# Eight projection chunks in three passes over split operands, and the modulation chunks moved with them

## The reference, cut to what matters

```python
hc = modulate(rms_norm(ctx, norm1_g[l]), csh1, csc1)
s_f, s_b = context_states(hc @ w_in[l][:, HG_KDIM:3 * HG_KDIM + HG_WIDTH], lbs[l])
hx = modulate(rms_norm(x, norm1_g[l]), sh1, sc1)
x_mix, _, _ = token_mixer(hx @ w_in[l], lbs[l], s_f, s_b, *mix_args)
...
q, z_f, z_b, vi, g, p_hy, g_logits = jnp.split(p, SPLIT_POINTS, axis=-1)
o, s_f, s_b = hgrn2_bidir(heads(q...), heads(vi...), fwd, bwd, s0_f, s0_b)   # scans both ways, chunks of 32
y_a = hgrn2_readout(o, g, hg_norm_g, p.dtype)
y_b = hyena_branch(p_hy, conv_w, conv_b, filt, d_skip)
return merge_branches(y_a, y_b, g_logits, w_pa, w_pb, w_o), s_f, s_b
```

## Time and profile before

| what | value |
|---|---|
| median of 3 runs | 2048.84 us (2046.73 to 2051.15) |
| profiled execution: span of its instructions | 2045.0 us |
| TensorE busy | 1947.3 us, 95% of the span |
| "projected", from chunk 4 on | 153.8 to 234.9 us |
| the two scans | 234.9 to 276.4 and 276.4 to 313.0 us |
| "hyena" | 313.0 to 374.2 us |

### The profile page before, as it was taken

One profiled execution on the slowest core, in us unless ns is written; L12 is line 12 of the kernel. 1 busy time (PEld: TensorE's weight loads), 2 busy tenths in 40 slices (PEclk: granted clock), 3 DMA queues, 4 the chain that ended last, 5 costly groups with the idle time before them and its releaser, 6 DMA issues.

```text
span 2045.0 us, 27442 instructions
## 1 busy us (share of the span) xinstructions
PE 1947.3 (95%) x11522; PEld 1406.8 (69%) x11522; DVE 727.9 (36%) x1213; ACT 610.7 (30%) x931; POOL 389.3 (19%) x205
## 2 busy tenths in 40 slices
PE   6999899999999999997999799999999999988998
PEld 2767696864444444446887557777777778678998
DVE  1624244232222222226243744222222535464333
ACT  2422102032222222223112534322223511545454
POOL 2000000020000000005001321433333310424764
PEclk9999999989999999998999899999999999989999
DMA  9469916549999999982222102544444223414551
GB/s 360 162 219 363 336 42 226 191 169 394 428 423 426 423 426 422 425 353 89 102 105 95 62 31 107 181 144 144 170 159 144 84 82 124 167 42 142 188 176 52
DMA packets 120213, 428.38 MB, mean 209 GB/s; under 512 B 5690, under 2 KB 23141, under 8 KB 107456
## 3 DMA queue, kind: packets, MB, share of 16 engines
q1 hardware_dynamic: 118016, 416.56, 52.8%
q0 software_dynamic: 2112, 10.57, 1.4%
HBM read 426.07 MB, written 1.05 MB: 209 GB/s over the span
## 4 chain that ended last, share of the span: by engine, by line
PE 64%; PEld 18%; issue 6%; DVE 3%; POOL 2%; ACT 2%; DMA 2%; PEldq 0%; DVEq 0%; POOLq 0%; SPq 0%; ACTq 0%
PE bank L527 63%; PEld bank L527 18%; PE bank L542 2%; DMA ring<-in_ada_w 1%; DMA ring<-in_w_in 1%; PEldq L506 0%; POOL arena L1815 0%; POOL arena L1814 0%; DVE H L1900 0%; DVE H_low L1907 0%; DVE arena L2399 0%; POOL arena L1819 0%; POOL arena L1817 0%; POOL arena L1820 0%; POOL arena_r L1855 0%
## 5 line engine op out<-in xcount | busy, mean ns | idle before, releaser
L527 PE MATMUL bank<-arena_r 128*128 128x512 f32 (+1 forms) x2112 | 599.0, 351 | 11.8 <-ACT arena_r L1332 5.4
L527 PE MATMUL bank<-arena_r,ring_low 128*128 128x512 f32 (+2 forms) x1792 | 561.7, 348 | 5.4 <-DVE H_low L1907 5.3
L527 PEld LDWEIGHTS bank<-arena_r 128*128 128x128 f32 x2112 | 374.1, 190 | 103.9 <-issue 47.7
L527 PEld LDWEIGHTS bank<-arena_r,ring_low 128*128 128x128 f32 (+1 forms) x1792 | 329.2, 189 | 51.5 <-issue 6.1
L527 PE MATMUL bank<-arena 128*128 128x64 bf16 (+8 forms) x2588 | 308.6, 285 | 25.3 <-DMA arena<-in_hy_filt_w 11.3
L527 PEld LDWEIGHTS bank<-arena 128*128 128x128 bf16 (+4 forms) x2588 | 190.3, 132 | 129.6 <-issue 93.4
L527 PE MATMUL bank<-ring,arena 128*64 128x512 f32 x1024 | 278.2, 595 | 1.1 <-ACT arena L1501 0.7
L527 PE MATMUL bank<-H_low,arena_r 128*128 128x512 f32 (+1 forms) x672 | 217.6, 341 | 0.0
L2455 DVE SCALAR_TENSOR_TENSOR X<-bank,mod,X 128x256 f32<-128x256 f32 x216 | 94.6, 479 | 314.2 <-PE bank L527 314.2
L1346 ACT ACTIVATE arena<-bank 128x512 f32<-128x512 f32 (+2 forms) x106 | 51.4, 496 | 410.2 <-PE bank L527 410.1
L1841 POOL TENSOR_TENSOR ring_low<-ring,arena_r 128x2048 fp32r<-128x2048 f32 x32 | 146.9, 4613 | 141.3 <-ACT arena_r L1691 70.8
...
## 6 DMA issues: line engine op xcount, KB each, us to landing
...
H<-in_moe_w_down SPq DMA_DIRECT2D x16, 2048.0 KB, 15.9
...
```

The lines of the kernel that those rows point to most:

```text
L527: ins = nc.tensor.matmul(o, l, r, start=start, stop=stop, skip_group_check=True)
```

## The change

Projection chunks 4 to 11 are also done in three passes over split operands. For chunks 4 to 7 ScalarE copies the high half of the chunk (two pieces of 2048 columns, `first_high`) into `W4h`, of which chunks 5, 6 and 7 share one buffer, and GpSimd subtracts it from the slot into `ring_low` (`first_low`). TensorE does all high passes of the four tiles of a chunk first, and then the low ones. For gate chunks 8 to 11 the high half goes into the `ring_low` buffer of the next slot number, so that a gate chunk takes two numbers of the ring (`gate_high`, `gate_low`, `chunk_used(2)`). The latents are kept as two halves, `HPX` (tokens, in `X_r`) and `HPC` (context, in `arena_r`); the copy `HX` is gone, and a k-step of the two wide chunks has five matmuls (four of 256 columns, one of 512) in place of three of 512 (`wide3`). Scan scratch moves to free `W4h`: `QD` is written over `LC`, and so waits for `ctx_arg`. The modulation chunks are grouped anew: 14 are behind chunks 1 to 7 (16 before), four behind gate chunk 10 in one row and two behind gate chunk 11. The start of `scan_prep` waits for the high passes of chunk 4. A few semaphores are merged and renamed, which changes no order.

```diff
-        ADA1, WIN, MERGE, MOE = 0, 4, 36, 40
+        ADA1, WIN, MERGE, MOE = 0, 4, 40, 44
...
-        BEHIND = [[], [0], [1, 2], [3, 4, 5], [6, 7], [8, 9], [10, 11, 12], [13, 14, 15]]
+        BEHIND = [[], [0, 1], [2, 3], [4, 5], [6, 7], [8, 9], [10, 11], [12, 13]]
+        GROUP = [(4, 6, 0, 8)] * 8 + [(5, 7, 8, 6)] * 6 + [(6, 6, 14, 6)] * 6
         ADA_COLS = 384
 
         def win(j):
 
-            return WIN + j + sum(len(b) for b in BEHIND[:j]) if j < 8 else WIN + (24, 25, 28, 30)[j - 8]
-
-        GATE_ADA = [WIN + 26, WIN + 27, WIN + 29, WIN + 31]
+            return WIN + j + sum(len(b) for b in BEHIND[:j]) if j < 8 else WIN + (22, 24, 26, 32)[j - 8]
+
+        GATE_ADA = {14: WIN + 28, 15: WIN + 29, 16: WIN + 30, 17: WIN + 31, 18: WIN + 34, 19: WIN + 35}
...
-                for i in BEHIND[j] if j < 8 else ([], [16, 17], [18], [19])[j - 8]:
-                    n += 1
+                for i in BEHIND[j] if j < 8 else ([], [], [14, 15, 16, 17], [18, 19])[j - 8]:
+                    n = n + 1 if j < 8 else GATE_ADA[i]
...
-        Hw = H[:, :, :].rearrange("p k n -> p (k n)")
-        QM, KM, QD = [[A3(off, HG_H, L), Hw[:, h:h + 1024].rearrange("p (a b) -> p a b", a=HG_H)]
-                      for off, h in ((15360, 0), (16384, 1024), (17408, 2048))]
-        SC = [A3(18432, 8, P), Hw[:, 3072:4096].rearrange("p (a b) -> p a b", a=8)]
+        QM = [A3(15360, HG_H, L), H[:, 0:HG_H, L:2 * L]]
+        KM = [A3(16384, HG_H, L), H[:, HG_H:2 * HG_H, L:2 * L]]
+        QD = LC
+        SC = [A3(18432, 8, P), A3(17408, 8, P)]
...
-        Hp = AR3(12288, KT, 2 * L)
+        HPX, HPC = Xr[:, :, L:2 * L], AR3(12288, KT, L)
+        Hp = lambda k, s: (HPX, HPC)[s][:, k, :]
...
+        W4h = [ar_r[:, 14336:18432], ar_r[:, 19456:23552]]
...
+            def wide3(o, w, k, start, stop, inc=None):
+
+                mm(o[:, 0:L], w[0], HPX[:, k, :], start, False)
+                mm(o[:, L:2 * L], w[0], HPC[:, k, :], False, False)
+                mm(o, w[0], Hl[:, k, :], False, False)
+                mm(o[:, 0:L], w[1], HPX[:, k, :], False, False)
+                mm(o[:, L:2 * L], w[1], HPC[:, k, :], False, stop, inc)
+
+            def behind(n, i):
+                g, bank, first, V = GROUP[i]
+                ada(n, g, bank, i - first, V, blk=min(i // 8, 1))
...
+            def high_passes(o, wh, nts, inc=None):
+                for nt in nts:
+                    for k in range(KT):
+                        last = (nt, k) == (nts[-1], KT - 1)
+                        mm(o[nt][:, 0:L], wh[:, k, nt * P:(nt + 1) * P], HPX[:, k, :], k == 0, False)
+                        mm(o[nt][:, 0:L], wh[:, k, nt * P:(nt + 1) * P], Hl[:, k, 0:L], False, False, inc if last else None)
+
+            def low_passes(o, wl, nts):
+                for nt in nts:
+                    for k in range(KT):
+                        mm(o[nt][:, 0:L], wl[:, k, nt * P:(nt + 1) * P], HPX[:, k, :], False, k == KT - 1,
+                           "tile_done" if k == KT - 1 else None)
+
+            for j in range(4, 8):
+                n = win(j)
+                pe.wait_ge(S("first_high"), 2 * (j - 4) + 2)
+                o = [tile_bank() for nt in range(4)]
+                high_passes(o, W4h[min(j - 4, 1)].rearrange("p (k n) -> p k n", k=KT), range(4), "high_used")
+                if j == 5:
+                    ada_turn(4, 6, 0, 8)
+                pe.wait_ge(S("first_low"), 2 * (j - 4) + 2)
+                low_passes(o, as_cols(n, slot=low), range(4))
+                chunk_used()
+                for i in BEHIND[j]:
+                    n += 1
+                    behind(n, i)
...
+            def gate_chunk(j):
+                return as_cols(win(j) + 1, slot=low), as_cols(win(j), slot=low)
+
             def gate_tile(j, nt):
-                n = win(j)
-                chunk_in(n)
+                wh, wl = gate_chunk(j)
                 o = tile_bank()
+                c = slice(nt * P, (nt + 1) * P)
                 for k in range(KT):
-                    mm(o[:, 0:L], as_cols(n)[:, k, nt * P:(nt + 1) * P], HX[:, k, :], k == 0, k == KT - 1,
-                       "tile_done" if k == KT - 1 else None)
+                    mm3(o[:, 0:L], (wh[:, k, c], wl[:, k, c]), (HPX[:, k, :], Hl[:, k, 0:L]), k == 0, k == KT - 1,
+                        "tile_done" if k == KT - 1 else None)
...
-            ada(GATE_ADA[1], 6, 6, 1, 4)
-            for nt in range(2):
-                gate_tile(10, nt)
-            pe.wait_ge(S("o_inverse"), 1)
+            gate_tile(10, 1)
+            pe.wait_ge(S("o_ready"), 2)
+            gate_tile(10, 2)
             pe.wait_ge(S("tables_in"), 32)
             pe.wait_ge(S("uv_ready"), 1)
             for tb in range(2):
                 for c in range(HYT):
                     tr(ps[4 + tb][:, c * P:(c + 1) * P], UV[:, c, tb * P:(tb + 1) * P], "tokens_turned" if c == 3 else None)
-            for nt in range(2, 4):
-                gate_tile(10, nt)
-            chunk_used()
-            ada(GATE_ADA[2], 6, 6, 2, 4)
+            gate_tile(10, 3)
+            chunk_used(2)
+            for i in range(14, 18):
+                behind(GATE_ADA[i], i)
             pe.wait_ge(S("un_ready"), 2)
             spectrum_half(0)
-            for nt in range(2):
-                gate_tile(11, nt)
+            pe.wait_ge(S("first_high"), 16)
+            o = [tile_bank() for nt in range(4)]
+            wh, wl = gate_chunk(11)
+            high_passes(o, wh, range(4))
             spectrum_half(1)
-            for nt in range(2, 4):
-                gate_tile(11, nt)
-            chunk_used()
-            ada(GATE_ADA[3], 6, 6, 3, 4)
...
+            def first_high(j):
+                n = win(j)
+                act.wait_ge(full[n % RING], arrived(n))
+                if j > 5:
+                    act.wait_ge(S("high_used"), j - 4)
+                    act.wait_ge(S("first_low"), 2 * (j - 4))
+                for a in range(2):
+                    s = slice(2048 * a, 2048 * (a + 1))
+                    A_(W4h[min(j - 4, 1)][:, s], slot(n)[:, s], ACT.Copy).then_inc(S("first_high"), 1)
+
+            def gate_high(j):
+                n = win(j)
+                act.wait_ge(full[n % RING], arrived(n))
+                act.wait_ge(used, n + 1 - RING + 1)
+                for a in range(2):
+                    s = slice(2048 * a, 2048 * (a + 1))
+                    A_(low(n + 1)[:, s], slot(n)[:, s], ACT.Copy).then_inc(S("first_high"), 1)
+
             for j, c in enumerate(WIN_ORDER[:8]):
+                if 4 <= j <= 6:
+                    first_high(j + 1)
                 for nt in range(4):
+                    if (j, nt) == (3, 2):
...
+            gate_high(8)
             for d in range(2):
                 for j in range(4):
                     act.wait_ge(S("turned"), 4 * d + j + 1)
                     o = (KDN, KEN)[j // 2][:, (j % 2) * 4:(j % 2) * 4 + 4, :]
                     A_(o, ps[j][:, :].rearrange("p (a b) -> p a b", a=4), ACT.Copy).then_inc(S("turned_out"), 1)
+                gate_high(9 + d)
...
+            def first_low(j):
+                n = win(j)
+                for a in range(2):
+                    s = slice(2048 * a, 2048 * (a + 1))
+                    pool.wait_ge(S("first_high"), 2 * (j - 4) + a + 1)
+                    G.tensor_tensor(low(n)[:, s], slot(n)[:, s], W4h[min(j - 4, 1)][:, s].bitcast(F32), ALU.subtract).then_inc(S("first_low"), 1)
+
+            def gate_low(j):
+                n = win(j)
+                for a in range(2):
+                    s = slice(2048 * a, 2048 * (a + 1))
+                    pool.wait_ge(S("first_high"), 2 * (j - 4) + a + 1)
+                    i = G.tensor_tensor(low(n)[:, s], slot(n)[:, s], low(n + 1)[:, s].bitcast(F32), ALU.subtract)
+                i.then_inc(full[(n + 1) % RING], 16)
+
+            for j in range(4, 7):
+                first_low(j)
             pool.wait_ge(S("ada_turned"), 5)
             bring(hmask, T["hg_mask"].rearrange("p (a b) -> p a b", a=2), "x_in")
+            first_low(7)
             phase_end(pool, "projected")
+            for j in range(8, 11):
+                gate_low(j)
             phase_end(pool, "scan_b")
             bring(A(15360, 2048), T["hy"][:, 0:2048], "tables_in")
+            gate_low(11)
...
+                dve.wait_ge(S("ctx_arg"), d + 1)
...
+                    dve.wait_ge(S("high_used"), 1)
+                    dve.wait_ge(S("first_low"), 2)
```

105 lines of the change are left out of this document (54 added, 51 removed).

## The result

The change makes the kernel slower: 2082.45 us (2076.2 to 2084.47, 4 runs) against 2047.79 us (2044.86 to 2051.15, 4 runs) before, a ratio of 1.0165 (95% interval 1.0142 to 1.0188), +34.7 us where +20.3 was predicted. The profiled execution has a span of 2082.7 us; from the first half of the merge on it does what the one before did, so the whole difference arises in the stretches that the prediction works through.

A forecast was written before the change was run, and what follows sets the result against it. TensorE, busy 95% of the span, was taken to bound the kernel. The terms 5.0 - 0.5 + 3.4 + 12.4 gave +20.3, a span of 2065.3 and, with 3.8, a time of 2069 us; range 2046 to 2080.

The forecast's parts named there:

- The 3.8 us: Outside the profiled span: what the median stands above it, added to the span of 2065.3 us to give 2069.
- scan 1 +3.4: Scan 1: VectorE's step 9 us late beside GpSimd, TensorE gets the state at 25, not 19.3; +3.4 us.
- each wait is followed by a slow clock that isn't absorbed: Slower rival, on TensorE's waits: four more slow clocks at 1.7 us, or worse transfer overlap; 2080 us, chance 8%.
- +5.0 predicted: "Projected": waits take the place of passes saved, so the stretch ends at 239.9 against 234.9 us.
- The wait before chunk 7: "Projected": TensorE waits 14.7 us for ScalarE's high copy, which stands behind the exponentials of scan 1.
- Without the hold: VectorE and GpSimd not delaying each other at their shared port pair: "projected" -5.6 us, the sum some 17 us less.
- Hyena, +12.4 predicted: Hyena: late ring transfers and a high copy move its last modulation chunk's end from 46.0 to 58.4 us.
- the three waits: Hyena: TensorE waits 3 to 5 us each, twice for modulation chunks' `ada_w` transfers, once for the high copy.
- Scan 0, -0.5 predicted: Scan 0: shorter gate quarters save time, against waits of 1.5 us for GpSimd and 0.5 for VectorE; -0.5 us.
- the rival that it costs nothing: In the chain of VectorE and GpSimd: VectorE goes first and GpSimd gives way; +2.8 us, 2051.7 us, chance 24%.
- Slower: The whole kernel: the outcome that its time rises, given a chance of 0.72, against same 0.15 and faster 0.13.
- The faster rival: Hyena: transfers land in time, decided at number 34, and VectorE isn't held up; 2038.4 us, chance 12%.

The follow-up runs named there:

- E4: The changed kernel with 28 filler matmuls on TensorE in scan 1, ahead of the third state, where it waited for VectorE; 2072.5 us, ratio 1.0116.
- E10: The changed kernel with filler matmuls ahead of TensorE's waits in "projected", scan 1 and hyena; 2075.6 us, ratio 1.0134.
- E1: The changed kernel with GpSimd's fourteen subtractions of chunks 5 to 11 cut from 2048 to 64 columns, low products left out; 2055.9 us, ratio 1.0039.
- E7: The changed kernel with all sixteen subtractions on VectorE instead of GpSimd, the result complete; 2058.4 us, ratio 1.0045.
- E12: The kernel before, fourteen modulation chunks in "projected", with the change's two ring numbers per gate chunk and hyena order, no copies or subtractions; 2047.7 us, ratio 1.0013.
- E14: E7 with two extra GpSimd subtractions of 2048 columns in scan 1, on a buffer nobody reads; 2063.0 us, ratio 1.0090.

## Why the prediction was right or wrong

Over the three profiles of the changed kernel, "projected" grew by 9.4, 8.3 and 8.9 us, scan 0 by 0.5, -1.0 and 0.6, scan 1 by 12.9, 8.5 and 11.0, hyena by 15.1, 14.7 and 14.6. The means, 8.9 + 0.0 + 10.8 + 14.8 = 34.5, make up the 34.7 us between the medians; the kernel before has one profile only. The direction and each mechanism were right; the sum was 14 us short, and the range ended 2.5 us below the result. The 3.8 us that the sum adds for what lies around the span are too many: the changed kernel's profiled execution took 2084.47 us at a span of 2082.7, 1.8 more, so 2 us of the 3.8 only say where one execution of the kernel before lay among its runs.

**The term that failed is "scan 1 +3.4".** VectorE was held, the state came late, and TensorE waited 6.0 us, where I had 5.7 (19.3 to 25). With that wait filled (E4) scan 1 grew by 4.1, nearly my number. But behind the pause TensorE ran at 1.2 GHz. The sum has a low clock only where a chunk stands behind a pause, at 1.7 us, and puts it at nothing in the scans; here it lasted 14 to 23 us behind the wait, and cost some 7 us of the missing 14. My rival "each wait is followed by a slow clock that isn't absorbed" had four waits at 1.7; E10 shows that the low clocks of hyena are absorbed after all, and E4 that the one in scan 1 is worth as much as those four (41.3 us against a mean of 47.9).

**"Projected", +5.0 predicted, +8.9 measured.** The wait before chunk 7 is 14.8 us for 14.7 predicted, for the reason given: E1 started it 8.2 us earlier (10.6 predicted). But it started at 225.8, 3.5 us later than predicted, and what followed took 0.9 more, as the low clock cost 2.5 us and not 1.7. Chunk 4 began at 153.3 instead of 151.7, which makes the wide k-steps 3.1 us and not the 1.5 chosen from 0 to 4, if all of it is theirs. Chunk 5's transfer landed 17.0 us after its issue, third in the queue (14.8 by 5.3 us each), and the chunk started at 177.1 and not at 172.8:

```profile
153.72 1.82 SPq L282 DMA_DIRECT2D ring<-in_w_in  x1
170.76 3.71 ACT L1457 ACTIVATE arena_r<-ring 128x2048 fp32r<-128x2048 f32 x2 [15.60 <-DMA ring<-in_w_in]
```

Without the hold I had the stretch end at 229.3. E1 ended it at 235.3 and E7 at 232.7, so the copies and the late start alone cost more than the sum gives them.

**Hyena, +12.4 predicted, +14.8 measured.** The places of the three waits are as predicted, and their releaser is the ring: the high copy of gate chunk 11 was ready at 39.2 us, not 37.1. Its transfer was issued at 354.1, 17.8 us into hyena (16.7 predicted), and landed 17.7 us later (16.7 predicted). E12 has the two waits for modulation chunks without any high copy or subtraction, and a hyena of 75.1, so it is the ring and not the copies that makes the loss.

**Scan 0, -0.5 predicted, 0.0 measured**, with a wait of 2.4 us for GpSimd's low half, 1.5 predicted.

**The hold.** Against the rival that it costs nothing (2051.7) stand E1, E7 and E14. The rule of the Trainium skill (SBUF — State Buffer, section "SBUF: two separate sides") that the engine which starts first keeps the shared port pair to its end fits the rows; ports themselves no row shows. The page also counts VectorE's 2-port performance modes among what needs the pair, and I had reckoned only with two inputs in SBUF. The row of L2133, one wide input and 4.11 us for 0.41, sides with the page, if it ran in such a mode, which no row tells. Without the hold I had the change at 2051.7; E1 gave 2055.9.

**The chances.** Slower had 0.72, and came. The faster rival fell at the place named: the modulation chunk of number 34 had TensorE wait 6.0 us.
